# Latent attention relaid: 128-partition query tiles, rotary parts apart, heads in pairs, attended tokens scaled instead of probabilities

## The chip, the cores and the metric

One core of a Trainium2 chip. The metric is the device time of one execution in microseconds. In the profile PE is TensorE (PEld its weight loads), DVE is VectorE, ACT is ScalarE, POOL is GpSimd and SP is SyncE.

## What is computed

A decoder trunk of two layers, 256 tokens by 1024 features, float32. In a layer one input projection feeds three token mixers (a gated linear recurrence called LRU, retention, latent attention); their outputs are projected, weighted by sigmoid gates, added and projected again. A gated MLP with a short convolution follows. The part in question:

```python
q = (rmsnorm(cq, q_norm_g) @ w_uq).reshape(bsz, s, 8, 96)          # 64 plain + 32 rotary per head
q_nope, q_rope = q[..., :64], apply_rope(q[..., 64:])
k_nope, v = split((rmsnorm(ckv, kv_norm_g) @ w_ukv).reshape(bsz, s, 8, 128))
k_rope = apply_rope(kr)                                            # one rotary key for all heads
p = softmax(mask(q @ k.T * 96 ** -0.5))                            # 2 query blocks of 128
o = p @ v
merged = gates[0] * y_lru + gates[1] * y_ret + gates[2] * (o @ mla_wo)
```

## The kernel before, in words

Each engine has its own instruction list, written out by hand, and semaphores tie them together; there is no planner. Both layers run the same list in a loop.

**Weights.** Every weight block (mostly 128 x 2048 numbers, 1 MB) goes through a ring of three slots. SP loads block j into `raw` when the split of block j-3 is done; ACT copies it to `w_hi` in a rounded format (`split_hi`, L543) once PE is done with block j-3; DVE writes the rest, raw minus hi, to `w_lo` (`split_lo`, L1007). PE then makes each product of three matmuls, hi by lo, lo by hi and hi by hi (`mm3`, L1469). POOL sums the conditioning weights beside that and PE takes its sums in `ada_part` (L1505).

**Latent attention, first part.** After the retention scores PE runs `uq(0)` and `uq(1)`: each head's 96 query columns are one weight tile, so the eight heads are 8 x 3 x 3 = 72 matmuls of 256 tokens, laid out as 96 partitions per head in `AB`. Then `uk` (keys, 64 of the 96 partitions in `CD`), `head_means` and `head_scales` (the norm of retention) and the values into `EF`. On DVE the LRU recurrence (four scans, L1256) stands between the retention scores and the split of the key/value weights.

**Latent attention, second part.** Twelve steps m follow, four for each of the mixers in the order retention, LRU, attention. `merge_gate(m)` makes gate logits (48 matmuls), `merge_product(m)` projects a mixer's output (24 matmuls). DVE joins them in `merge(m)` (L1349, L1354). PE may overwrite the product's bank only after the merge of the step before (`mg_y`). Steps 0 to 7 also carry one attention head each, in this order on PE:

```python
for m in range(1, HEADS):
    merge_gate(m)            # m > 1
    mla_transpose(m - 1)     # waits for softmax_norm(m - 1) on ACT
    mla_score(m)
    merge_product(m)
    mla_av(m - 1)
```

The rotation of q and k is five float32 matmuls with a rotation matrix (`q_rotate(0..3)`, L1833, and `key_rotate`, L1757) around gates 0 and 1. DVE multiplies by the sine and cosine tables and adds, on 32 partitions, three operations of 512 numbers for each of the four pairs of heads (L1282, L1283, L1286), and `mla_score(0)` waits for the last. For each head DVE adds the mask (L1327), takes two maxima (L1329, L1330) and scales them (L1332); ACT takes the exponentials (L805, L807), DVE the reciprocal of the sums (L1337), ACT scales the probabilities (L813, L814), PE transposes three 128 x 128 tiles (L1773), ACT copies them out (L820), and `mla_av` (L1784, L1785) moves the probabilities past the values, so that the output has features on partitions. A float32 matmul is two instructions in the trace, a float32 transpose one.

ACT's and DVE's lists in a step m are the gate's tanh (L800), the softmax pieces, then the splits of the blocks three ahead. Block numbers: 15, 16 are uq, 17 is the key/value weights, 18 gate 0, 19 product weights 0, 20 gate 1, 21 gate 2, 22 product weights, 23 gate 3, 24 gate 4, 25 the product weights of the LRU, 26 gate 5 and so on, three blocks for two steps. In step 1 DVE also writes the low part of the LRU's output, `ob_lo` (L1387), which `merge_product(4)` waits for.

Of the kernel before, what the change touches and what calls it, by code (L numbers as in the profile page):

```python
# [21 lines left out]
P = 128  # L22
# [67 lines left out]
def trunk_kernel(nc, A, consts, out):  # L90
# [80 lines left out]
    with ctx:  # L171
# [38 lines left out]
        mx = sb("mx", [P, 2, 8])  # L210
# [101 lines left out]
        kr_ev, c_sq = sig("kr_ev", 1), sig("c_sq", 3)  # L312
# [3 lines left out]
        uq_ps, uq_ev = sig("uq_ps", 2), sig("uq_ev", 4)  # L316
        uk_ps, uk_ev = sig("uk_ps", 2), sig("uk_ev", 2)
        uv_ps, uv_ev = sig("uv_ps", 1), sig("uv_ev", 2)
        kt_ps, kt_t, kt_c, kt_sum, kt = sig("kt_ps", 1), sig("kt_t", 1), sig("kt_c", 1), sig("kt_sum", 1), sig("kt", 2)
        qt_ps, qt_t, qt_c, qt = sig("qt_ps", 4), sig("qt_t", 4), sig("qt_c", 4), sig("qt", 4)  # L320
        s_ps, s_m, s_max, s_neg = sig("s_ps", 8), sig("s_m", 8), sig("s_max", 8), sig("s_neg", 8)
        s_e, s_rc, s_n, s_tp, s_tev, s_av = (sig(n, 8) for n in ("s_e", "s_rc", "s_n", "s_tp", "s_tev", "s_av"))
# [24 lines left out]
        def gate_bank(m):  # L347

            return (3, 5)[m] if m < 2 else (4, 6)[m % 2]
# [6 lines left out]
        def kv_parts(t, j, packed):  # L356
# [7 lines left out]
            return [v[:, :, :, i] for i in range(2)]  # L364

# [138 lines left out]
        def _(act):  # L504
# [40 lines left out]
            def split_block(l, j):  # L545
# [9 lines left out]
                elif j == J[("ukv", 0)]:  # L555
# [4 lines left out]
                    a.then_inc(hi_ready.s, 1)  # L560
                elif j < NM:
# [80 lines left out]
            with act.Fori(0, L) as l:  # L642
# [49 lines left out]
                A_(kr[:], PS[:, 2, T:2 * T], ACT.Copy).then_inc(kr_ev.s, 1)  # L692
# [36 lines left out]
                def q_out(i):  # L729

                    if i % 2 == 0:
                        act.wait_ge(uq_ps.s, uq_ps.at(l, i // 2 + 1))
                    else:
                        product_done(act, l, J[("uq", i // 2)])
                    A_(AB[0:DQK, 2 * i:2 * i + 2, :].rearrange("p a b -> p (a b)"), PS[0:DQK, (2, 4, 6, 3)[i], :],
                       ACT.Copy).then_inc(uq_ev.s, 1)
# [8 lines left out]
                q_out(1)  # L745
                split_block(l, 18)
                ret_out(1)
                act.wait_ge(cn_lo.s, cn_lo.at(l, 1))
# [3 lines left out]
                q_out(2)  # L752
                q_out(3)
                split_block(l, 19)
                for i in range(2):
                    act.wait_ge(rv_ps.s, rv_ps.at(l, i + 1))
                    A_(var_sd[:, i, :], PS[:, (1, 2)[i], 0:8], ACT.Sqrt, bias=eps).then_inc(rv_sd.s, 1)

                def k_out(i):

                    act.wait_ge(uk_ps.s, uk_ps.at(l, i + 1))
                    for b in range(2):
# [1246 lines left out]
```

## Time and profile before

| | us |
|---|---|
| runs | 1103.14 median (1101.35 to 1103.78), 3 runs |
| the profiled execution | 1100.68, its span 1099.0 |
| PE busy | 1001.4 |
| DVE busy | 785.1 |
| ACT busy | 543.3 |
| POOL busy | 535.8 |
| mean granted TensorE clock | 0.974 of 2.4 GHz |

A matmul's row lasts until its result is out, so neighbouring matmuls overlap in the trace; the distance from start to start is what a matmul costs. In the windows, "PE busy" is the time covered by at least one of them, and the window's length minus that is PE's idle time.

### The profile page before, as it was taken

What the parts mean: (1) busy time and instruction counts of PE and PEld (TensorE: products, weight loads), DVE (VectorE), ACT (ScalarE), POOL (GpSimd) and SP (SyncE); (2) the same over time, 40 slices, a digit from 0 to 9 for tenths busy, and PEclk for the clock granted to TensorE, in tenths of its full rate; (3) what the DMA queues carried; (4) which work ended last, traced back from release to release, by engine and by line L of the source; (5) the groups of instructions that cost most, each with busy time, mean ns of one, the idle gap of its engine ahead of it and who ended that gap; (6) DMA issues with size and microseconds to landing.
All of it is one profiled execution on the core that took longest, in us unless ns stands there. A gap on an engine that the chain in (4) does not pass through costs nothing.

```text
span 1099.0 us, 19161 instructions
## 1 busy us (share of the span) xinstructions
PE 1001.4 (91%) x7074; PEld 927.4 (84%) x7074; DVE 785.1 (71%) x847; ACT 543.3 (49%) x697; POOL 535.8 (49%) x365
## 2 busy tenths in 40 slices
PE   5799999889998899999958999988999879999996
PEld 5789998788886899999947999878889769999995
DVE  4867678765678688888765867876666868766755
ACT  1543656545445555545444365744443564454554
POOL 0385675356664348888881477535566524000000
PEclk9999999999999799999988999999999979999998
DMA  9867655356555468677643765534665635555430
GB/s 300 306 192 239 210 187 184 108 173 210 168 196 192 134 219 264 227 247 227 232 156 106 231 198 177 191 115 154 205 194 187 220 110 179 192 178 187 169 115 39
DMA packets 140456, 206.56 MB, mean 188 GB/s; under 512 B 6289, under 2 KB 113115, under 8 KB 140251
## 3 DMA queue, kind: packets, MB, share of 16 engines
q1 hardware_dynamic: 128000, 161.76, 45.6%
q0 software_dynamic: 11520, 41.95, 11.2%
q10 hardware_dynamic: 859, 1.81, 0.4%
q8 instruction: 51, 0.84, 0.3%
q14 instruction: 26, 0.21, 0.1%
HBM read 204.45 MB, written 1.05 MB: 187 GB/s over the span
## 4 chain that ended last, share of the span: by engine, by line
PE 74%; DVE 12%; ACT 6%; issue 6%; DMA 1%; SPq 0%; DVEq 0%; ACTq 0%
PE banks L1469 63%; ACT w_hi L543 2%; PE banks L1495 2%; DMA AB<-in_ada_w 1%; DVE w_lo L1007 1%; PE banks L1520 1%; PE banks L1505 1%; DVE h L1058 1%; DVE AB L1283 1%; DVE mx L1332 1%; DVE h_lo L1065 1%; DVE x L1086 1%; PE banks L1587 1%; PE banks L1765 1%; ACT pbuf L807 1%
## 5 line engine op out<-in xcount | busy, mean ns | idle before, releaser
L1469 PE MATMUL banks<-h_lo,w_hi 128*128 128x256 f32 x1504 | 435.5, 290 | 7.9 <-DVE h_lo L1065 7.9
L1469 PE MATMUL banks<-h_hi,w_lo 128*128 128x256 f32 x1504 | 427.7, 284 | 0.0
L1469 PE MATMUL banks<-h_hi,w_hi 128*128 128x256 f32 x1504 | 427.5, 284 | 0.0
L1007 DVE TENSOR_TENSOR w_lo<-raw,w_hi 128x2048 fp32r<-128x2048 f32 (+1 forms) x87 | 244.9, 2820 | 84.4 <-ACT w_hi L543 84.2
L1469 PEld LDWEIGHTS banks<-h_lo,w_hi 128*128 128x128 f32 x1504 | 290.7, 193 | 12.1 <-issue 11.0
L1469 PEld LDWEIGHTS banks<-h_hi,w_lo 128*128 128x128 f32 x1504 | 290.9, 193 | 1.6 <-issue 1.4
L1469 PEld LDWEIGHTS banks<-h_hi,w_hi 128*128 128x128 f32 x1504 | 290.7, 193 | 0.0
L462 POOL TENSOR_TENSOR adp<-adw,cact 128x1024 f32<-128x1024 f32 x80 | 191.3, 2391 | 36.8 <-DMA adw<-in_ada_w 17.3
L543 ACT ACTIVATE w_hi<-raw 128x2048 fp32r<-128x2048 f32 (+1 forms) x87 | 162.2, 1873 | 64.7 <-PE banks L1469 57.4
L473 POOL TENSOR_TENSOR adacc<-adp 128x256 f32<-128x256 f32 x40 | 42.8, 1070 | 255.4 <-PE banks L1505 252.5
L1427 DVE TENSOR_TENSOR w_lo<-raw,w_hi 128x2048 fp32r<-128x2048 f32 x56 | 133.1, 2377 | 17.1 <-ACT w_hi L892 16.7
L468 POOL TENSOR_TENSOR adp<-adp 128x512 f32<-128x512 f32 x80 | 137.7, 1721 | 3.0 <-POOL adp L462 1.4
L1404 DVE SCALAR_TENSOR_TENSOR EF<-banks,cur,EF 128x254 f32<-128x254 f32 (+1 forms) x176 | 76.8, 478 | 75.5 <-ACT EF L873 71.3
L892 ACT ACTIVATE w_hi<-raw 128x2048 fp32r<-128x2048 f32 x56 | 107.2, 1913 | 46.3 <-PE banks L1469 46.3
L450 POOL DMA_DIRECT2D adw<-in_ada_w x80 | 63.1, 789 | 91.8 <-POOL adp L462 50.3
L873 ACT ACTIVATE EF<-banks,cur 128x256 f32<-128x256 f32 x88 | 44.9, 560 | 124.3 <-PE banks L1469 124.3
L1469 PE MATMUL banks<-w_hi,oa_lo 128*128 128x512 f32 x208 | 82.7, 398 | 2.7 <-DVE oa_lo L1422 2.7
L1469 PE MATMUL banks<-w_lo,oa_hi 128*128 128x512 f32 x208 | 82.2, 395 | 0.0
L1469 PE MATMUL banks<-w_hi,oa_hi 128*128 128x512 f32 x208 | 82.1, 395 | 0.0
L477 POOL TENSOR_TENSOR adp<-adp 128x256 f32<-128x256 f32 x40 | 52.6, 1315 | 3.1
L1469 PEld LDWEIGHTS banks<-w_hi,oa_lo 128*128 128x128 f32 x208 | 39.1, 188 | 12.0 <-DVE oa_lo L1422 3.6
L479 POOL TENSOR_TENSOR adacc<-adacc,adp 128x256 f32<-128x256 f32 x40 | 47.2, 1181 | 3.1
(273 smaller groups left out, 1503.0 us busy)
## 6 DMA issues: line engine op xcount, KB each, us to landing
raw<-in_w_in SPq DMA_DIRECT2D x52, 1024.0 KB, 6.4
raw<-in_ffn_w_up SPq DMA_DIRECT2D x44, 1024.0 KB, 5.8
adw<-in_ada_w POOLq DMA_DIRECT2D x80, 512.0 KB, 4.1
raw<-in_ffn_w_down SPq DMA_DIRECT2D x22, 1024.0 KB, 5.0
raw<-in_w_out SPq DMA_DIRECT2D x8, 1024.0 KB, 7.2
raw<-in_ret_wo SPq DMA_DIRECT2D x4, 1024.0 KB, 7.2
raw<-in_lru_wo SPq DMA_DIRECT2D x4, 1024.0 KB, 5.8
raw<-in_mla_wo SPq DMA_DIRECT2D x4, 1024.0 KB, 5.1
```

The lines of the kernel that those rows point to most:

```text
L450: pool.dma_start(adw[:, half], src(g)[:, 4 * half:4 * half + 4, :]).then_inc(adw_in[half], 16)
L462: nc.gpsimd.tensor_tensor(adp[:], weights, cb, ALU.mult).then_inc(ad_op, 1)
L468: nc.gpsimd.tensor_tensor(adp[:, 0:2], adp[:, 0:2], adp[:, 2:4], ALU.add).then_inc(ad_op, 1)
L477: nc.gpsimd.tensor_tensor(adp[:, 0], adp[:, 0], adp[:, 1], ALU.add).then_inc(ad_op, 1)
L479: nc.gpsimd.tensor_tensor(adacc[:, b], adacc[:, b], adp[:, 0], ALU.add).then_inc(acc_ready, 1)
L543: A_(dst, src, ACT.Copy).then_inc(hi_ready.s, 1)
L873: a = A_(EF[:, 2 * part + b, :], PS[:, 4 + part, T * b:T * b + T], ACT.Identity, scale=cur[:, bass.ds(i * 2 + col["tap2"] + NFF * (1 - par ...
L892: A_(w_hi[:, slot, :], raw[:, slot, :], ACT.Copy).then_inc(hi_ready.s, 1)
L1007: V.tensor_tensor(dst, whole, hi, ALU.subtract).then_inc(lo_ready.s, 1)
L1404: v = V.scalar_tensor_tensor(EF[:, 2 * part + b, d:T], PS[:, 4 + part, T * b:T * b + T - d], cur[:, bass.ds(i * 2 + col[f"tap{tap}"] + NFF ...
L1427: V.tensor_tensor(w_lo[:, slot, :], raw[:, slot, :], w_hi[:, slot, :].bitcast(F32), ALU.subtract).then_inc(lo_ready.s, 1)
L1469: ins = MM(ps, lhs, rhs, start=first and n == 0, stop=last and n == 2)
```

## The change

The query weights are packed as they are split: a block of four heads becomes 256 plain columns (four heads by 64) and 128 rotary columns (the two odd heads, then the two even ones), so a block is three tiles of 128. `AB[:, 0:4]` holds the plain parts, `AB[:, 4:6]` the rotary parts of all eight heads; `CD[:, 0:4]` the plain keys, `kr` the rotary key in all four groups of 32 partitions, and the values move to `CD[:, 4:8]`. A head's score is the sum of a 64-row matmul and a 32-row matmul. Heads go in pairs. The values are now the moving operand and the probabilities the weights, so the output has tokens on partitions; it is scaled by the reciprocal sums on DVE once, and transposed at the end (`mla_features`).

On PE, in order (L numbers are those of the kernel before where a line is kept):

```diff
@@ PE, first part
                 two_tiles(l, J[("g", 0)], 4)
+                pe.wait_ge(kt_t.s, kt_t.at(l, 1))
+                MM(PS[:, 2, 0:T], rot_m, lat[:, 0, :], start=True, stop=True).then_inc(kt_ps.s, 1)
...
-                pe.wait_ge(kr_ev.s, kr_ev.at(l, 1))
+                pe.wait_ge(kt.s, kt.at(l, 1))
                 two_tiles(l, J[("g", 1)], 2)
...
-                    for pair in range(2):
-                        n = 2 * i + pair
-                        sg, cnt = ((g_ev, 2), (lg_ev, 1), (lg_ev, 2), (ry_ev, 1))[n]
-                        pe.wait_ge(sg.s, sg.at(l, cnt))
-                        for b in range(2):
-                            cols = slice(DQK * (2 * pair + b), DQK * (2 * pair + b) + DQK)
-                            for k in range(QK):
...
+                    for t in range(3):
+                        ps = PS[:, (2, 6)[i], T * t:T * t + T] if t < 2 else PS[:, 4, T * i:T * i + T]
+                        cols = slice(P * t, P * t + P)
+                        for k in range(QK):
...
                 uk(1)
+                pe.wait_ge(qt_c.s, qt_c.at(l, 1))
+                pe.wait_ge(qt_t.s, qt_t.at(l, 1))
+                MM(PS[:, 4, :], rot_m, rot_tmp.rearrange("p a b -> p (a b)"), start=True, stop=True).then_inc(qt_ps.s, 1)
                 head_means(1)
@@ PE, second part
+                def mla_scores(p):
+                    if p >= 1:
+                        pe.wait_ge(s_tev.s, s_tev.at(l, p))
+                    for qs, ks, out_cols in ((slice(0, P), slice(0, P), slice(0, P)), (slice(P, T), slice(0, T), slice(P, 3 * P))):
+                        for h in (2 * p, 2 * p + 1):
+                            r = slice(64 * (h % 2), 64 * (h % 2) + 64)
+                            MM(PS[:, (3, 4)[h % 2], out_cols], AB[r, h // 2, qs], CD[r, h // 2, ks], start=True, stop=False)
+                        for h in (2 * p, 2 * p + 1):
+                            r = rope_rows(h)
+                            ins = MM(PS[:, (3, 4)[h % 2], out_cols], AB[r, 4 + h // 4, qs], kr[r, ks], start=False, stop=True)
+                    ins.then_inc(s_ps.s, 1)
+                def mla_av(p):
+                    pe.wait_ge(s_tev.s, s_tev.at(l, p + 1))
...
+                    for h in (2 * p, 2 * p + 1):
+                        pt, cols = ptb[:, h % 2, :], slice(64 * h, 64 * h + 64)
+                        MM(PS[:, 1, cols], pt[:, 0:P], v[:, 0, cols], start=True, stop=True)
+                        MM(PS[:, 2, cols], pt[:, P:2 * P], v[:, 0, cols], start=True, stop=False)
+                        ins = MM(PS[:, 2, cols], pt[:, 2 * P:3 * P], v[:, 1, cols], start=False, stop=True)
...
                 merge_gate(0)
-                key_rotate()
-                q_rotate(0)
-                q_rotate(1)
                 merge_gate(1)
-                q_rotate(2)
-                q_rotate(3)
                 merge_product(0)
...
+                mla_scores(0)
+                merge_product(1)
+                ada_part(ada_n, 6)
+                for m in range(2, HEADS):
+                    merge_gate(m)
+                    if m % 2 == 0:
+                        mla_transpose(m // 2 - 1)
+                        merge_product(m)
+                        mla_av(m // 2 - 1)
                     else:
+                        mla_scores(m // 2)
                         merge_product(m)
                         ada_part(ada_n, 6 + m // 2)
 
                 m = HEADS
                 merge_gate(m)
-                mla_transpose(m - 1)
-                mla_av(m - 1)
+                mla_transpose(3)
+                mla_av(3)
                 merge_gate(m + 1)
+                mla_features(0)
+                mla_features(1)
```

On DVE the scans leave the first part, the key is rotated before block 13's split, one `rotary_q_parts` and `rotary_q_sum` of 128 x 512 take the place of the twelve operations on 32 partitions, and the list of the steps becomes (`softmax_scores` is the mask add over both heads, two maxima over both, one scaling; `attended_low` reads the transposed output from the banks):

```diff
                 for m in range(12):
                     j = J[("gate", 0, 0)] + 3 * (m // 2)
-                    if 1 <= m < HEADS:
-                        softmax_scores(m)
...
+                    if m % 2 == 1 and m < HEADS:
+                        softmax_scores(m // 2)
+                    if m == 8:
+                        attended(0)
+                        attended(1)
+                        attended_low(0)
+                        attended_low(1)
+                    if m % 2 == 0:
                         split_block(l, j + RING)
+                    if m == 0:
+                        for t in range(4):
+                            lru_scan(t)
                     merge(m)
...
                     if m % 2 == 1:
                         split_block(l, j + RING + 1)
-                    if m % 2 == 1:
                         split_block(l, j + RING + 2)
-                    if m == 1:
-                        dve.wait_ge(l_ohi.s, l_ohi.at(l, 1))
...
+                    if m == 0:
+                        lru_out()
+                    if m == 3:
+                        lru_low()
```

On ACT the copy of `kr` (L692), two of the four query copies and two of the four key copies, the two broadcasts of the rotary key into `CD` (L789) and the scaling of the probabilities (L813, L814) go; both `uq` blocks are split in three pieces each instead of one (on DVE too). In the steps:

```diff
                     gate(m)
-                    if 1 <= m <= HEADS:
-                        transposed(m - 1)
-                    if m < HEADS:
-                        softmax_exp(m)
-                    if m in (5, 8):
-                        attended(m // 4 - 1)
+                    if m % 2 == 0 and 2 <= m <= HEADS:
+                        transposed(m // 2 - 1)
+                    if m % 2 == 1 and m < HEADS:
+                        softmax_exp(m // 2)
+                    if m == 9:
+                        attended(0)
+                        attended(1)
                     if m % 2 == 0:
                         split_block(l, j + RING)
                     else:
                         split_block(l, j + RING + 1)
-                    if m < HEADS:
-                        softmax_norm(m)
-                    if m % 2 == 1:
                         split_block(l, j + RING + 2)
+                    if m == 2:
+                        lru_high()
```

`softmax_exp(p)` is four exponentials, two for each head of the pair; `transposed(p)` copies 128 x 768 from two banks in one instruction.

## Rows read from the trace of the kernel before

**Rows 1.** The page: the span and the busy line of part 1.
```profile
span 1099.0 us, 19161 instructions
PE 1001.4 (91%) x7074; PEld 927.4 (84%) x7074; DVE 785.1 (71%) x847; ACT 543.3 (49%) x697; POOL 535.8 (49%) x365
```

**Rows 2.** Windows, layer 0 attention (the last: both together in layer 1).
```profile
core 0: us, PE busy (x) PEld busy (x) DVE busy (x) ACT busy (x) POOL busy (x), PEclk, DMA share, GB/s
162.70:183.75 21.05, 20.35 (x150) 17.62 (x149) 18.76 (x18) 13.39 (x20) 8.58 (x8) 1.00 0.61 200
183.75:309.08 125.33, 112.35 (x857) 104.30 (x856) 81.65 (x91) 57.41 (x91) 65.37 (x45) 0.99 0.50 163
212.51:239.65 27.14, 23.21 (x173) 21.85 (x172) 16.04 (x20) 13.53 (x24) 13.84 (x9) 0.94 0.63 195
688.41:834.71 146.30, 132.47 (x1004) 122.05 (x1003) 100.45 (x108) 70.68 (x110) 75.04 (x53) 0.99 0.53 169
```

**Rows 3.** Timeline of PE in layer 0: start, length; in brackets the idle time before.
```profile
203.52 0.49 PE L1764 MATMUL banks<-CD,AB 96*128 96x128 f32 x2 [1.35 <-DVE AB L1286]
...
210.12 0.55 PE L1773 MATMUL banks<-cst,pbuf 128*128 128x128 f32 x3 [2.80 <-ACT lat L800]
...
232.95 0.91 PE L1773 MATMUL banks<-cst,pbuf 128*128 128x128 f32 x3 [3.93 <-ACT pbuf L814]
...
305.78 0.39 PE L1469 MATMUL banks<-oa_lo,w_hi 128*128 128x256 f32 x1 [0.78 <-DVE EF L1354]
```

**Rows 4.** Critical chain, layer 0, pieces in order: start, length, what.
```profile
100.89 0.86 PE banks L1587 x2
...
136.56 2.32 PE banks L1650 x20
...
146.33 0.64 PE banks L1626 x4
146.97 0.22 PE banks L1627 x4
147.19 5.95 PE banks L1469 x48
...
245.65 0.33 PE banks L1773 x3
...
281.78 0.22 PE banks L1764 x2
282.00 0.43 PE banks L1765 x2
282.43 2.80 PE banks L1469 x24
285.24 0.58 PE banks L1784 x2
285.81 0.22 PE banks L1785 x2
...
286.57 5.88 PE banks L1469 x48
```

**Rows 5.** DVE, groups by line and form, 162 to 310 us.
```profile
L1007 DVE TENSOR_TENSOR w_lo<-raw,w_hi 128x2048 fp32r<-128x2048 f32 x16 | 43.4, 2715 | 16.6 <-ACT w_hi L543 16.6
...
L1256 DVE TENSOR_TENSOR_SCAN EF<-grow,h 128x256 f32<-128x256 f32 x4 | 4.8, 1256 | 0.0
...
L1327 DVE TENSOR_TENSOR pbuf<-banks,cst 128x384 f32<-128x384 f32 x8 | 4.5, 556 | 9.9 <-PE banks L1765 9.7
L1354 DVE SCALAR_TENSOR_TENSOR EF<-lat,banks 128x512 f32<-128x512 f32 x6 | 4.1, 682 | 8.2 <-PE banks L1469 8.2
...
L1387 DVE TENSOR_TENSOR ob_lo<-EF,ob_hi 128x1024 fp32r<-128x1024 f32 x1 | 1.7, 1749 | 0.0
```

**Rows 6.** ACT, the same stretch.
```profile
L543 ACT ACTIVATE w_hi<-raw 128x2048 fp32r<-128x2048 f32 x17 | 32.4, 1904 | 6.9 <-PE banks L1469 6.9
...
L807 ACT ACTIVATE pbuf<-pbuf,mx,lat_rc 128x256 f32<-128x256 f32 x8 | 4.7, 586 | 0.0
```

More of the change, by code:

```diff
@@ L784, in _ @@
                     A_(flat2(oa_hi, i), flat2(tmp, i), ACT.Copy).then_inc(r_ohi.s, 1)
-                k_out(1)
-                act.wait_ge(kt_sum.s, kt_sum.at(l, 1))
-                for half in range(2):
-                    A_(CD[64:96, 4 * half:4 * half + 4, :], kr[64:96, :].unsqueeze(1).to_broadcast([32, 4, T]),
-                       ACT.Copy).then_inc(kt.s, 1)
                 def gate(m):
@@ L822, in attended, with softmax_exp @@
-                def attended(i):
-                    act.wait_ge(s_av.s, s_av.at(l, 4 * i + 4))
-                    if i == 0:
-                        product_done(act, l, J[("gate", 0, 3)])
-                    A_(flat2(oa_hi, i), PS[:, 2, :], ACT.Copy).then_inc(m_ohi.s, 1)
+                def softmax_exp(p):
+                    act.wait_ge(s_neg.s, s_neg.at(l, p + 1))
+                    for b in range(2):
+                        for c, cols in enumerate((slice(0, P), slice(P, 3 * P))):
+                            a = A_(pbuf[:, b, cols], pbuf[:, b, cols], ACT.Exp, scale=lat_rc[:, c:c + 1],
+                                   bias=sneg[:, c, b:b + 1], accum_out=ssum[:, c, 2 * p + b:2 * p + b + 1])
+                    a.then_inc(s_e.s, 1)
@@ new lines, in transposed, with attended @@
+                def transposed(p):
+                    act.wait_ge(s_tp.s, s_tp.at(l, p + 1))
+                    if p >= 1:
+                        act.wait_ge(s_av.s, s_av.at(l, p))
+                    A_(ptb[:], PS[:, 3:5, 0:384], ACT.Copy).then_inc(s_tev.s, 1)
+                def attended(c):
+                    act.wait_ge(m_tp.s, m_tp.at(l, c + 1))
+                    product_done(act, l, J[("gate", 0, 3)])
+                    A_(oa_hi[:, :, P * c:P * c + P], PS[:, (3, 4)[c], :].rearrange("p (a b) -> p a b", a=4),
+                       ACT.Copy).then_inc(m_ohi.s, 1)
@@ L828, in merged_hi, with lru_high @@
+                def lru_high():
+                    act.wait_ge(l_o.s, l_o.at(l, 1))
+                    A_(ob_hi[:, 0:4, :], EF[:, 4:8, :], ACT.Copy).then_inc(l_ohi.s, 1)
                 def merged_hi(i):
@@ new lines, in lru_out, with lru_low @@
+                def lru_out():
+                    dve.wait_ge(l_h.s, l_h.at(l, 4))
+                    dve.wait_ge(lg_ev.s, lg_ev.at(l, 2))
+                    V.tensor_tensor(EF[:, 4:8, :], EF[:, 4:8, :], EF[:, 0:4, :], ALU.mult).then_inc(l_o.s, 1)
+                def lru_low():
+                    dve.wait_ge(l_ohi.s, l_ohi.at(l, 1))
+                    V.tensor_tensor(ob_lo[:, 0:4, :], EF[:, 4:8, :], ob_hi[:, 0:4, :].bitcast(F32),
+                                    ALU.subtract).then_inc(l_olo.s, 1)
@@ L1788, in merge_y, with mla_features @@
+                def mla_features(c):
+                    pe.wait_ge(s_n.s, s_n.at(l, c + 1))
+                    o = AB[:, 4 + 2 * c:6 + 2 * c, :].rearrange("p a b -> p (a b)")
+                    for t in range(4):
+                        ins = nc.tensor.transpose(PS[:, (3, 4)[c], P * t:P * t + P], o[:, P * t:P * t + P], ident)
+                    ins.then_inc(m_tp.s, 1)
                 def merge_y(b, i, wj):
```

311 lines of the change are left out of this document (138 added, 173 removed).

## The prediction

> **What bounds the kernel.** PE is busy for 91% of the span [rows 1], so I looked for the time in which it is not, stage by stage. In the windows of the attention stage [rows 2], the first part of layer 0 takes 21.05 us with 0.70 idle, the second part 125.33 us with 125.33 - 112.35 = 12.98 idle. Layer 1's whole stage takes 146.30 us, against 21.05 + 125.33 = 146.38 in layer 0, so each number below counts twice. The timeline shows where PE waits [rows 3]: 1.35 us for the last rotation of q on DVE, 2.80 us in step 1 for the first head's softmax, 3.93 us in step 3 for ACT's scaled probabilities, and 0.78 us for the merge of step 8, four of the eight waits in it. After the wait of 3.93 us the granted clock fell: the window 212.51 to 239.65 has 0.94 [rows 2], that is some 3.3 us at 1.2 instead of 2.4 GHz, in which half the work was done, a loss of 1.6 us. So besides its work the second part loses 12.98 + 1.6 = 14.6 us per layer. Outside this stage the change touches nothing but the rotary key.
>
> **The prices of PE's work** [rows 4]. A 256-token matmul of `mm3` costs 5.88 / 48 = 0.12 us (24 of a product, 2.8 us). A float32 rotation of 512 columns costs 0.86 us, a transpose 0.33 / 3 = 0.11. One head's score of 96 rows costs 0.22 + 0.43 = 0.65 us. Two heads' retention scores, with the same 384 columns each but on 64 rows at different partitions, cost 0.64 + 0.22 = 0.86 together, not 1.3: they run beside each other in part, down to 0.86 / 8 = 0.108 us an instruction. The gate behind them took 5.95 instead of 5.88 us, which I take for the change of tile, 0.09 us with rounding.
>
> **The change, part by part, per layer.** (minus is a gain)
> - Query projection: 72 matmuls become 2 x 3 x 9 = 54. 18 x 0.12 = -2.2 us.
> - Rotation of q: four matmuls become one, -3 x 0.86 = -2.6. The key's matmul only moves ahead.
> - Scores: eight times 0.65 (5.2 us) become four pairs of 16 instructions, half on 64 and half on 32 rows. No row shows 32-row tiles. If each pair of tiles runs fully side by side a pair costs 2 x 0.65 = 1.3 us; if nothing does, 4 x 0.65 + 4 changes of tile x 0.09 = 3.0. The nearest row is retention's: 16 x 0.108 = 1.7 and 0.36 for the changes, 2.1 us. 4 x 2.1 - 5.2 = +3.2.
> - Values: a head costs 0.58 + 0.22 = 0.80 us now, 6.4 in all. After it, each head is six instructions with full weights and 64 moving columns; the nearest row, with one column, has 2.32 / 20 = 0.116 us. 48 x 0.116 = 5.6. That is -0.8; between instructions of 0.10 and 0.15 the total is 4.8 to 7.2.
> - `mla_features`: eight transposes, +0.9. The softmax's 24 transposes stay.
> Together 2.2 + 2.6 + 0.8 - 3.2 - 0.9 = 1.5 us less work.
>
> **The waits.** I walk through the lists with durations from the rows, from PE's view.
> First part: the scans leave DVE (4 x 1.2 us [rows 5]), so the key/value split is early; the rotary parts of q (two operations of about 0.7) follow uq(1) and are needed only behind 12 + 12 + the key matmuls and a head mean, 4.6 us later. Hidden. Idle 0.70 becomes about 0.4. The three-piece splits of uq cost perhaps 0.5 us more on ACT and DVE, hidden behind the two-tile products of 5.95 us. The rotary key's two products and sum (0.4 us each) go into DVE's wait for the next block and behind the retention scores; PE needs the sum only after 20 small matmuls of 2.32 us [rows 4]. If that cover were gone they would cost 1.2.
> - Gate 0 to scores: q and k are long ready; 1.35 us goes.
> - Product 1 waits for merge(0), and on DVE that now stands behind block 21's split and the four scans. From gate 0's end: tanh 0.6, high part 1.9 [rows 6], low part 2.7 [rows 5], scans 4.8, merge 0.7 [rows 5]: 10.7 us. PE gets there after gate 1, product 0, scores: 5.9 + 2.8 + 2.1 = 10.8. On the edge; I count 0.3.
> - Step 1's wait of 2.80 goes, since the softmax of a pair now has a product and a gate as cover (2.8 + 5.9 us against about 2.3 on DVE and 2.2 on ACT). Product 2 then waits for block 22: 0.5.
> - Step 3's wait of 3.93 goes too, since no scaling on ACT stands between. **But a new one comes at product 4.** It needs `ob_lo` (`lru_low`), which is now last in DVE's step 3, behind the splits of blocks 25 and 26. From the end of product 3: the scores ended 2.9 us before it, DVE's part for the pair takes 2.3 (the mask add of 768 numbers about 0.95, from 0.556 for 384 [rows 5], maxima 1.1, scaling 0.2), ACT's four exponentials 2.2 (0.59 for the longer [rows 6]): +1.6. High part of 25 at 3.5, low parts 2.7 each to 6.2 and 8.9, `lru_low` 1.75 to 10.7. PE arrives after 0.5 of `ada_part`, 5.9 of gate 4 and 0.7 of transposes: 7.1. The wait is 3.6 us, like today's 3.93, so I count the clock loss of 1.6 us again.
> - Step 8: the values of the last pair wait for ACT's copy of 768 columns, 0.8. Merge(8) stays at 0.8, gate 9 may wait 0.2.
> Sum: 0.3 + 0.5 + 3.6 + 0.8 + 0.2 + 0.8 = 6.2 idle and 1.6 for the clock, 7.8 against 14.6. With 0.3 from the first part, -7.1 us.
>
> Per layer 1.5 + 7.1 = 8.6 us, twice 17.2. The profiled execution had 1100.7 us, which gives 1083.5; it lies 2.5 us under the median of the three runs, which would give 1085.9. I say **1084.5 us**.
>
> ACT loses sixteen scalings and the broadcasts of a layer, DVE nine of the twelve operations of the rotation. That is worth only what it does to the waits above; it is not added. The transfers are not in the way: the second part uses 0.50 of the DMA engines [rows 2], and at some 9 us less it would use 0.54.
>
> **A rule that speaks against it.** The gate behind 64-row scores lost 0.09 us [rows 4], and the sum goes by that. The Trainium skill, "TensorEngine Tiling (Array Packing)", section "Key Properties", says that changing the tiling mode, not just the tile, drains TensorE. By that rule the four changes in each pair's scores would each wait for the matmul before to come out.
>
> **Rivals.**
> 1. More is gained (15%). The two heads' tiles run fully beside each other (1.3 a pair, -3.2 a layer) and splits a few tenths shorter than their mean leave under 3 us of wait at product 4, with no fall of the clock (-2.5). For it: retention's pairs overlap, and the wait of 2.80 us was followed by matmuls at full clock. Against: 0.108 us an instruction looks like a floor. 1084.5 - 2 x 5.7 = 1073.
> 2. Less is gained (15%). The 32-row tiles do not overlap with anything (+3.6 a layer) and the DVE chain ahead of product 4 and product 1 runs 1 us later each (the 2.7 us of a split is a mean, and several stand in a row), +2. 1084.5 + 11 = 1096.
> 3. The stage is bound by the supply of split blocks, not by the softmax (4%): every gate would wait for its block and the saved time would come back as waits for `w_lo`. DVE is busy 81.65 of 125.33 us [rows 2], against it. 1101 to 1105.
> 4. Slower (6%): each change between 128-, 64- and 32-row tiles drains the array. The place is `mla_scores`, four changes in each of eight pairs, 32. To cancel 17.2 us each would have to cost 0.54 us more than the 0.09 I count. At one matmul's whole latency (a row lasts some 0.3 us from start to end [rows 3]: 0.39 for the first) it is 32 x 0.3 = 10 us, still 1094; the two-pass float32 tiles would have to drain between each other too, 128 times at 0.15 = 19, which gives 1104 to 1108.
>
> **How the numbers follow.** The forecast has 60%, with its own range 1079 to 1091 (clock fall or not, 3; values and scores to either side, 3 to 5). The range of 1074 to 1096 takes in most of rivals 1 and 2 and leaves about 2 in 10 out. A measurement of this kernel tells 0.2%, 2.2 us, from no change: faster 0.90, same 0.04, slower 0.06.
>
> **What would show it.** Right: the sum of PE's idle time in the second part near 6 us, one wait of 3 to 4 us before product 4 released by DVE's `ob_lo`, no wait before the first scores, some 2.1 us per pair of scores, uq in 3.3 us each, about 8 us less from uq(0) to gate 10 in each layer. Wrong: waits of over 1 us before other products, released by `w_lo` or by merges; a pair of scores over 3 us; a clock under 0.9 in a window where it was 1.00.

## The result, and the profile of the changed kernel

The changed kernel takes 1082.86 us, the median of four runs (1081.25 to 1085.35), where the kernel before, run beside it, takes 1102.7. The ratio is 0.9826, with a 95% interval of 0.9813 to 0.9839: faster by 1.7%. The forecast was 1084.5. The profiled execution had 1083.08 us and a span of 1081.4. The page begins with the span, then busy time by engine, then the shares of the chain that ended last:

```profile
span 1081.4 us, 19149 instructions
PE 997.6 (92%) x7138; PEld 928.0 (86%) x7138; DVE 765.2 (71%) x795; ACT 522.5 (48%) x651; POOL 555.3 (51%) x365
...
PE 82%; DVE 9%; ACT 4%; issue 3%; DMA 1%; SPq 0%; DVEq 0%; ACTq 0%
```

Beside [rows 1], PE's busy time fell by only 3.8 us of the 17.6 that the span lost. DVE lost 20 and ACT 21 us of work, while POOL's same 365 instructions took 19.5 us longer. So most of the gain, 13.8 us, is idle time of PE.

The windows of the stage from uq(0) to gate 10, the first and second part in layer 0, then all of it in layer 1 (columns as in [rows 2]):

```profile
165.57:184.50 18.93, 18.91 (x134) 16.09 (x132) 14.16 (x16) 12.01 (x16) 11.38 (x8) 1.00 0.73 242
184.50:302.69 118.19, 110.56 (x902) 105.43 (x902) 75.38 (x59) 48.09 (x68) 77.50 (x49) 0.99 0.54 174
680.70:817.81 137.11, 129.48 (x1034) 121.69 (x1033) 90.64 (x74) 60.10 (x83) 88.66 (x57) 0.99 0.56 182
```

Layer 0 takes 18.93 + 118.19 = 137.12 us instead of 146.38, layer 1 137.11 instead of 146.30: 9.3 and 9.2 us less. The idle time of the second part is 118.19 - 110.56 = 7.63 instead of 12.98, that of the first 0.02 instead of 0.70. The whole span splits without a rest: uq(0) starts 2.87 us later, layer 0's stage is 9.26 shorter, the stretch from there to layer 1's uq(0) 1.32 shorter (379.33 to 378.01), layer 1's stage 9.19 shorter, the end 0.70 shorter; together -17.60. Of the 2.87 us, some 0.9 come before any edit, and 0.4 to 0.6 are the rotary key's matmul, which now stands there. Most of the rest is a slower clock that layer 0 alone shows: the window from 140 to 160 us has a granted clock of 0.92 where the kernel before had 1.00, and layer 1 loses nothing there.

The timeline of PE in layer 0, with all waits of the second part:

```profile
201.70 0.39 PE L1503 MATMUL banks<-oa_lo,w_hi 128*128 128x256 f32 x1 [0.47 <-DVE h L1386]
...
213.21 0.38 PE L1503 MATMUL banks<-oa_lo,w_hi 128*128 128x256 f32 x1 [1.53 <-DVE w_lo L1018]
...
239.31 0.58 PE L1503 MATMUL banks<-ob_lo,w_hi 128*128 128x256 f32 x1 [3.95 <-DVE ob_lo L1299]
...
285.63 0.44 PE L1819 MATMUL banks<-CD,ptb 128*128 128x64 f32 x2 [0.90 <-ACT ptb L827]
...
299.74 0.39 PE L1503 MATMUL banks<-oa_lo,w_hi 128*128 128x256 f32 x1 [0.78 <-DVE EF L1391]
```

They stand before product 1, product 2, product 4, the values of the last pair and product 9, and sum to 7.63 us. The waits for q, for the first head's softmax and for the scaled probabilities [rows 3] are gone; the merge's 0.78 is as it was. Layer 1 has the same five (0.49, 1.50, 3.95, 0.90, 0.78). After the long one the clock fell. This is the window of product 4's matmuls, where a product at full clock takes 2.94 us:

```profile
239.31:243.59 4.28, 4.28 (x24) 4.28 (x25) 2.51 (x1) 0.00 (x0) 3.75 (x2) 0.65 1.00 296
```

And this is one pair's scores on PE, then the first matmul of the next product:

```profile
223.31 0.49 PE L1801 MATMUL banks<-CD,AB 64*128 64x128 f32 x4
223.73 0.49 PE L1804 MATMUL banks<-kr,AB 32*128 32x128 f32 x4
224.15 0.70 PE L1801 MATMUL banks<-CD,AB 64*128 64x256 f32 x4
224.79 0.70 PE L1804 MATMUL banks<-kr,AB 32*128 32x256 f32 x4
225.42 0.38 PE L1503 MATMUL banks<-oa_lo,w_hi 128*128 128x256 f32 x1
```

The starts are to be read here, since a duration has the array's latency in it: 225.42 - 223.31 = 2.11 us a pair, as forecast. What the 2.11 is made of is another matter, and took three runs.

### The profile page after: what moved, and what is told of

It is laid out like the page before. It is cut to its first block, busy times and chain, and to the rows that moved or that the text cites. A ratio compares the mean times of both kernels' runs of the same rounds, so it can differ in the third digit from the quotient of the medians.

```text
span 1081.4 us, 19149 instructions
## 1 busy us (share of the span) xinstructions
PE 997.6 (92%) x7138; PEld 928.0 (86%) x7138; DVE 765.2 (71%) x795; ACT 522.5 (48%) x651; POOL 555.3 (51%) x365
## 4 chain that ended last, share of the span: by engine, by line
PE 82%; DVE 9%; ACT 4%; issue 3%; DMA 1%; SPq 0%; DVEq 0%; ACTq 0%
PE banks L1503 70%; DVE w_lo L1018 2%; PE banks L1529 2%; ACT w_hi L565 1%; DMA AB<-in_ada_w 1%; DVE EF L1290 1%; PE banks L1554 1%; DVE h L1074 1%; PE banks L1539 1%; DVE h_lo L1081 1%; ACT pbuf L819 1%; DVE x L1102 1%; PE banks L1621 1%; PE banks L1640 1%; PE banks L1804 1%
## 5 line engine op out<-in xcount | busy, mean ns | idle before, releaser
L1018 DVE TENSOR_TENSOR w_lo<-raw,w_hi 128x2048 fp32r<-128x2048 f32 x83 | 237.1, 2872 | 69.6 <-ACT w_hi L565 69.3
L565 ACT ACTIVATE w_hi<-raw 128x2048 fp32r<-128x2048 f32 x83 | 156.8, 1907 | 70.8 <-PE banks L1503 60.8
L1461 DVE TENSOR_TENSOR w_lo<-raw,w_hi 128x2048 fp32r<-128x2048 f32 x56 | 133.1, 2376 | 17.3 <-ACT w_hi L903 16.8
L490 POOL TENSOR_TENSOR adp<-adp 128x512 f32<-128x512 f32 x80 | 134.3, 1678 | 3.0 <-POOL adp L484 1.4
L903 ACT ACTIVATE w_hi<-raw 128x2048 fp32r<-128x2048 f32 x56 | 107.1, 1913 | 46.6 <-PE banks L1503 46.6
L499 POOL TENSOR_TENSOR adp<-adp 128x256 f32<-128x256 f32 x40 | 61.2, 1530 | 3.1
L813 ACT ACTIVATE lat<-banks 128x512 f32<-128x512 f32 x24 | 14.4, 598 | 98.4 <-PE banks L1503 98.3
L501 POOL TENSOR_TENSOR adacc<-adacc,adp 128x256 f32<-128x256 f32 x40 | 59.7, 1493 | 3.1
```

The lines of the kernel that those rows point to most:

```text
L490: nc.gpsimd.tensor_tensor(adp[:, 0:2], adp[:, 0:2], adp[:, 2:4], ALU.add).then_inc(ad_op, 1)
L499: nc.gpsimd.tensor_tensor(adp[:, 0], adp[:, 0], adp[:, 1], ALU.add).then_inc(ad_op, 1)
L501: nc.gpsimd.tensor_tensor(adacc[:, b], adacc[:, b], adp[:, 0], ALU.add).then_inc(acc_ready, 1)
L565: A_(dst, src, ACT.Copy).then_inc(hi_ready.s, 1)
L903: A_(w_hi[:, slot, :], raw[:, slot, :], ACT.Copy).then_inc(hi_ready.s, 1)
L1018: V.tensor_tensor(dst, whole, hi, ALU.subtract).then_inc(lo_ready.s, 1)
```

## The experiments

The theory: each wait of the second part is set by one late operation in the queues of DVE or ACT, and the long one takes the clock with it; PE's work does the rest. The rival: DVE and ACT bound this part together and hand a removed wait on. "Stage" below is uq(0) to gate 10, 137.1 us in both layers of the changed kernel.

**The low part of the recurrent output one step earlier.**

```diff
-                    if m == 3:
+                    if m == 2:
                         lru_low()
```

> The changed kernel with one line moved: DVE's lru_low, the low part of the LRU's output, goes from the end of step 3 to the end of step 2, where DVE idles for 6 us. Theory (PE's walk sets the end; what product 4 waits for is its place in DVE's list): the wait of 3.95 us before product 4 and the slow clock behind it (24 matmuls in 4.45 instead of 3.1 us) go in both layers, 2 x (3.95 + 1.35) = 10.6 us, 1082.9 to about 1072. Block 25's low part ends 1.2 us before PE arrives, so it does not take the wait over. Rival (the stage is bound by the supply of split blocks): product 4 or a later product waits for w_lo in its place, and the time stays within 2 us of 1083.

Measured: 1074.37 us, 0.9739 of before (0.9704 to 0.9774); the stages take 131.56 and 131.48 us. Product 4 follows the transposes at once:

```profile
233.93 0.82 PE L1811 MATMUL banks<-cst,pbuf 128*128 128x128 f32 x6
234.50 0.36 PE L1503 MATMUL banks<-ob_lo,w_hi 128*128 128x256 f32 x1
```

The 24 matmuls take 2.94 us. The other four waits are as before (0.48, 1.52, 0.90, 0.78). The wait and the clock's loss sum to 3.95 + 1.34 to 1.51 = 5.3 to 5.5 us, and the stages are 5.6 us shorter each. So the new wait was real, nothing took its place, and it cost 11.2 us in the two stages. By the medians the kernel gains 8.5 us, 2 less than the forecast; at least part of that stands behind layer 1's stage, where the profiled execution took 1.9 us longer for the same work (265.5 against 263.6 us).

**Three more rotations of q.**

```diff
+                for _ in range(3):
+                    MM(PS[:, 4, :], rot_m, rot_tmp.rearrange("p a b -> p (a b)"), start=True, stop=True)
                 MM(PS[:, 4, :], rot_m, rot_tmp.rearrange("p a b -> p (a b)"), start=True, stop=True).then_inc(qt_ps.s, 1)
```

> The changed kernel with the rotation matmul of q written four times instead of once (the same result, as often as the kernel before rotates). Theory (PE's work in the first part is on the path to the end): 3 x 0.86 = 2.6 us more per layer, 1082.9 to about 1088. Rival (the work saved there is covered by what PE waits for afterwards): 0 to 1 us more.

Measured: 1088.32 us, 0.9866 (0.9837 to 0.9894). The stages take 139.66 and 140.61 us. In layer 0 that is 3 x 0.86 = 2.6 more; layer 1 has 0.8 us on top, where product 4 took 5.28 instead of 4.45 us at the slow clock (the profiled execution, 1092.69 us, was the longest of the four). The rotations' price is on PE's path in full.

**Probabilities scaled again.** ACT scales a pair's probabilities between its two splits of blocks, the transposes wait for that, and the later scaling on DVE is by one.

```diff
                         split_block(l, j + RING + 1)
+                        if m < HEADS:
+                            softmax_norm(m // 2)
                         split_block(l, j + RING + 2)
...
                 def mla_transpose(p):
-                    pe.wait_ge(s_e.s, s_e.at(l, p + 1))
+                    pe.wait_ge(s_nm.s, s_nm.at(l, p + 1))
```

> The changed kernel with the probabilities scaled again: for each pair DVE takes the reciprocals after the merge, ACT scales the four pieces between the splits of the two blocks, the transposes wait for that; the attended tokens are multiplied by one, so that work is the same. Theory (the pairs have a product and a gate as cover; the scaling's removal alone is worth little): ACT's 1.8 us per pair delays the second block of a step, so product 4 waits some 1.5 us longer and gate 9 some 0.5, the transposes of step 2 some 0.2: 1 to 2.5 us per layer, 1085 to 1088. Rival (taking the scaling off the way to the transposes is the main source of the gain): the waits of 2.8 and 3.9 us before transposes come back, 8 us or more in all, 1091 or more.

Measured: 1083.39 us, 0.9827 (0.9793 to 0.986), and the same five waits, product 4's at 3.97, in stages of 137.3 and 137.1 us. Both expectations were too high: the scaling costs nothing here. I looked for why, since 1.5 us of ACT work ahead of block 26's split should have made the low part of the recurrent output later. The timeline of DVE in the changed kernel (without the scaling), the low parts of blocks 25 and 26:

```profile
231.84 2.29 DVE L1018 TENSOR_TENSOR w_lo<-raw,w_hi 128x2048 fp32r<-128x2048 f32 x1 [2.61 <-ACT w_hi L565]
...
234.05 3.37 DVE L1018 TENSOR_TENSOR w_lo<-raw,w_hi 128x2048 fp32r<-128x2048 f32 x1
```

and POOL's operation beside the second:

```profile
233.27 2.00 POOL L490 TENSOR_TENSOR adp<-adp 128x512 f32<-128x512 f32 x1
```

The same operations with the scaling, where all times lie 0.93 us earlier:

```profile
234.09 2.40 DVE L1029 TENSOR_TENSOR w_lo<-raw,w_hi 128x2048 fp32r<-128x2048 f32 x1 [0.90 <-ACT w_hi L566]
...
232.33 2.01 POOL L491 TENSOR_TENSOR adp<-adp 128x512 f32<-128x512 f32 x1
```

Without the scaling the low part starts 0.9 us sooner and then stands: it takes 3.37 us and ends 2.15 us after POOL's sum (235.27 to 237.42). With it, it starts when the sum is nearly over, takes 2.40 us, and ends 2.15 us after it as well (234.34 to 236.49). The delay on ACT fell into time in which DVE could not work anyway. That fits the Trainium skill, "SBUF — State Buffer", section "SBUF: two separate sides", which calls the port pair that VectorE and GpSimd share an exclusive lock. The two ends at 2.15 us agree with it, and so does the whole trace of the changed kernel: 67 low parts of 2048 numbers begin during a sum of POOL, at any point of it, and all end 2.15 to 2.25 us after it, while the 45 that touch none take 2.28 or 2.29 us. It works the other way too: POOL's 256-column sums (L499, L501) that begin during a low part end 0.6 us after it, and there are 26 of these instead of 16, which is where POOL's longer busy time comes from (61.2 + 59.7 us instead of 52.6 + 47.2). Eight more low parts begin 0.01 to 0.56 us ahead of a sum of POOL and still end 2.16 us after it, so by the records it is not always the one that starts first that runs first. No run here moved POOL's work by itself.

**The four scans ahead of the split of block 17, as they were.**

```diff
+                for t in range(4):
+                    lru_scan(t)
                 split_block(l, 17)
                 split_block(l, 18)
...
-                    if m == 0:
-                        for t in range(4):
-                            lru_scan(t)
                     merge(m)
```

> The changed kernel with the four LRU scans back in front of the split of the key/value weights, as in the kernel before. Theory: product 1 no longer waits for merge(0) (0.47 us per layer), but in the first part the key/value split, the rotary parts of q and the variances come up to 4.8 us later, beyond their cover: waits of 1 to 2 us per layer before the keys, the rotation or the head scales. In sum 0.5 to 3 us slower, 1083.5 to 1086. Rival (the scans' place decides the first part, where the kernel before had them too): 1081 to 1083, no wait in the first part over 0.7.

Measured: 1086.52 us, 0.9849 (0.982 to 0.9877). The first part now waits 1.39 us for the key/value split and 1.24 for the rotary q, and the waits before product 1 and product 2 are gone. In layer 1 it waits once, 2.08 us, for the same split. So moving the scans is worth 3.7 us by the medians, a little over what I expected, though it also makes the 0.47 and part of the 1.53 us. The idle time of the stages hardly differs, 8.28 and 7.73 us against 7.65 and 7.63; what makes them longer, 138.87 and 140.19 us, is mostly the clock. Product 4 took 5.28 us in layer 0, and behind the 2.08 us of layer 1 the window of 10 us has a granted clock of 0.66.

**The exponentials behind the split.**

```diff
-                    if m % 2 == 1 and m < HEADS:
-                        softmax_exp(m // 2)
...
                         split_block(l, j + RING + 1)
+                        if m < HEADS:
+                            softmax_exp(m // 2)
                         split_block(l, j + RING + 2)
```

> In the odd steps ACT makes the high part of the first block ahead of the pair's exponentials. Theory: DVE's low part of that block starts up to 1.9 us earlier, so the wait of 1.5 us before product 2 goes, and that before product 4 stays or falls by up to 1 us, since the second block's low part starts where it does now: 2 x 1.5 to 2 x 2.5, 1078 to 1080 us. Rival (the transposes become late because the exponentials end 1.9 us later): a wait before the transposes of pairs 0 to 2, and 1083 us or more.

Measured: 1080.45 us, 0.9796 (0.9777 to 0.9815). Product 2's wait is gone and product 4's is 3.72, 1.76 us less idle; but product 4 took 5.28 us, 1.0 and 0.8 more at the slow clock, so the stages end at 136.34 and 136.03. No wait came before the transposes: the exponentials have slack.

**A shorter cover for the softmax.**

```diff
                 for m in range(2, HEADS):
-                    merge_gate(m)
                     if m % 2 == 0:
                         mla_transpose(m // 2 - 1)
+                    merge_gate(m)
+                    if m % 2 == 0:
                         merge_product(m)
```

> On TensorE the transposes of pairs 0, 1 and 2 stand ahead of the next gate instead of behind it, so that only a product and a part of ada (3.4 us) cover a pair's softmax (some 4.5 us from the end of the scores to the last exponential). Theory (the cover that the pairs' order gives is what removed the softmax waits): a wait of 1.0 to 1.5 us for the probabilities before each of the three. In the steps of pairs 0 and 1 it only takes the place of the wait that product 2 and product 4 have anyway, for blocks whose times hang on DVE; pair 2 has none to take: 1.2 us a layer, 1085.5 us. Rival (waits add up): 2 x 3 x 1.2, 1090 us. If no wait appears before the transposes, the cover by the gate wasn't needed.

Measured: 1089.13 us, 0.9878 (0.9857 to 0.9899), nearer the rival's figure. The waits of its second part up to the last pair:

```profile
198.88 0.39 PE L1503 MATMUL banks<-oa_lo,w_hi 128*128 128x256 f32 x1 [0.47 <-DVE h L1386]
204.70 0.88 PE L1811 MATMUL banks<-cst,pbuf 128*128 128x128 f32 x6 [2.35 <-ACT pbuf L819]
...
227.91 0.87 PE L1811 MATMUL banks<-cst,pbuf 128*128 128x128 f32 x6 [1.22 <-ACT pbuf L819]
237.18 0.38 PE L1503 MATMUL banks<-ob_lo,w_hi 128*128 128x256 f32 x1 [2.64 <-DVE ob_lo L1299]
...
255.58 0.87 PE L1811 MATMUL banks<-cst,pbuf 128*128 128x128 f32 x6 [1.22 <-ACT pbuf L819]
```

The mechanism is as expected. A wait of 2.35, 1.22 and 1.22 us came before each transpose; it took the place of product 2's wait and of 1.3 us of product 4's, and only the third was all new. The sum of waits is 9.58 instead of 7.63 us, and the stages take 139.06 and 139.16, 2.0 more each. That is 4 of the 6 us. The rest lies outside the stage: this execution began 2.6 us earlier with uq(0) and then needed 382.84 us from gate 10 to layer 1's uq(0), where the changed kernel needed 378.01 for the same work. Two windows of 20 us at the same distance behind gate 10, first of the changed kernel, then of this one:

```profile
322.69:342.69 20.00, 20.00 (x88) 16.07 (x87) 18.14 (x11) 8.98 (x10) 11.85 (x8) 1.00 0.71 230
642.69:662.69 20.00, 20.00 (x163) 19.31 (x161) 14.59 (x14) 14.74 (x26) 14.63 (x11) 1.00 0.47 149
```

```profile
322.05:342.05 20.00, 20.00 (x81) 15.97 (x80) 15.85 (x9) 8.99 (x10) 11.85 (x8) 0.91 0.73 239
642.05:662.05 20.00, 20.00 (x157) 19.28 (x156) 13.57 (x13) 18.05 (x28) 14.29 (x10) 0.97 0.58 181
```

PE is busy throughout in all four, but the granted clock is 0.91 and 0.97 here and 1.00 there. The edit does not reach this place, and the kernels compared below have 378 to 383 us there too. Within the stage the verdict is plain: without the gate as cover, softmax waits return; with it there are none.

**64 rows for the rotary products.** The 32-row matmuls become 64-row ones, so each score also has another head's rotary product in it.

```diff
-                            r = rope_rows(h)
+                            r = slice(64 * (h % 2), 64 * (h % 2) + 64)
```

> Changed computation: the rotary product of a head's scores runs over 64 rows instead of 32, so a score also has another head's rotary product in it; the number of instructions and columns is unchanged, and no change between 64 and 32 rows is left (the changes between 128 and 64 rows stay). My forecast's step counted 0.36 us a pair for four changes of tile: two of them would go, 8 pairs x 0.18 = 1.4 us, 1081.5 us in all. Reading of the trace after the change (each instruction of 128 columns takes 0.105 us on 64 and on 32 rows alike): nothing, 1083 us, and a pair still takes 2.11 us. Rival (a change of the row height drains the array at 0.3 us or more): 8 x 4 x 0.3 = 5 us less in total at least, 1078 or under.

Measured: 1086.2 us, 0.9836 (0.9808 to 0.9864), not told apart from the changed kernel. But a pair is much shorter:

```profile
222.35 0.49 PE L1801 MATMUL banks<-CD,AB 64*128 64x128 f32 x4
222.67 0.39 PE L1804 MATMUL banks<-kr,AB 64*128 64x128 f32 x4
222.90 0.60 PE L1801 MATMUL banks<-CD,AB 64*128 64x256 f32 x4
223.33 0.60 PE L1804 MATMUL banks<-kr,AB 64*128 64x256 f32 x4
223.86 0.38 PE L1503 MATMUL banks<-oa_lo,w_hi 128*128 128x256 f32 x1
```

1.51 instead of 2.11 us. Both readings of my own (two changes at 0.09 us, and no cost at all) were wrong, the second most of all. The rival's was right: eight pairs save 4.8 us of PE's time, near its 5, though the product written there, 8 x 4 x 0.3, is 9.6. The whole gained nothing: of 4 x 0.6 = 2.4 us a layer, 0.6 came back as a longer wait at product 1 (1.08 instead of 0.47) and 0.8 to 1.0 as a longer stretch of slow clock at product 4 (5.24 us at a granted 0.51). Each stage is 0.8 to 0.9 us shorter, and the stretch between the two 4.6 us longer, as in the run before.

This run had undone two things: the change of row height, and that a head's rotary rows lie in the other half of the partitions than its plain rows. Two runs told these apart.

**The halves.** Both parts of a head in the same half, 64 and 32 rows kept.

```diff
-                odd, even = (v[:, :, 2 * P + 64 * i:2 * P + 64 * i + 64].rearrange("p k (h n) -> p k h n", h=2) for i in range(2))
+                odd, even = (v[:, :, 2 * P + 64 * i:2 * P + 64 * i + 64].rearrange("p k (h n) -> p k h n", h=2) for i in (1, 0))
...
-            r = (64 if h % 2 == 0 else 0) + 32 * (h % 4 // 2)
+            r = 64 * (h % 2) + 32 * (h % 4 // 2)
```

> In the changed kernel a head's rotary rows (32) lie in the other half of the partitions than its plain rows (64). The run with 64-row rotary matmuls took 1.51 us a pair instead of 2.11, but it had undone two things: the change of row height and that change of half. Here the heights stay (64 and 32 rows), and the packed columns of the query weights and the rows are swapped so that both parts of a head lie in the same half; what is computed is the same. If the change of height costs (0.2 us each, three in a pair beside the one behind it): 2.11 us a pair still, 1083 us. If the change of half costs, because a head's second matmul then waits for the first of the other tile: 1.5 us a pair, 8 x 0.6 = 4.8 us less work, of which at least 0.6 a layer comes back as a wait at product 1: 1079 to 1080 us.

Measured: 1083.09 us, 0.9837 (0.9807 to 0.9866). A pair still starts 2.11 us before what follows (222.59 to 224.70). The half does not matter. On top of the best kernel (below) the same swap says the same:

> The same swap on top of the kernel with the three changes of order (1068.7 us), which has no waits left that would take the gain up but 0.9 and 0.8 us a layer. Height reading: 1068.7 us, 2.11 us a pair. Half reading: 1.5 us a pair, 4.8 us less, 1064 us, a little more if product 1 waits for the first merge again.

Measured: 1071.37 us, 0.9716 (0.9699 to 0.9732), 2.11 us a pair, stages of 129.02 and 129.09, as without the swap (129.03 and 129.08). The 2.7 us between the two medians are not in the stages; in the profiled executions, 1.7 us apart, uq(0) starts 1.9 us later with the swap.

**The three orders together.** The low part after product 2, the exponentials behind the split (both as above), and the first merge ahead of the last scan:

```diff
                     if m == 0:
-                        for t in range(4):
+                        for t in range(3):
                             lru_scan(t)
                     merge(m)
+                    if m == 0:
+                        lru_scan(3)
```

> Three changes of order in the queues of the second part: the low part of the recurrent output after product 2 instead of product 3, the high part of the odd steps' first block ahead of the exponentials on ACT, the first merge ahead of the last scan on DVE. Theory (the waits of 3.95, 1.5 and 0.47 us a layer are each set by one late operation, and the fall of the clock to 1.2 GHz goes with the wait of 3.95): 2 x (3.95 + 1.35 + 1.5 + 0.47) = 14.6 us less than the changed kernel, 1068.5 us; waits of 0.9 before the last pair's values and 0.8 before product 9 stay. Rival (DVE and ACT are the bound of this part and hand the waits on): only the 8.7 us that the move of the low part alone gave, 1074 us, with waits of 1 us or more before gates or products 6 and 8.

Measured: 1068.7 us, 0.9687 (0.9667 to 0.9707), against an expected 1068.5. Its windows, the stage's two parts in layer 0:

```profile
162.95:181.88 18.93, 18.93 (x135) 16.40 (x134) 14.47 (x16) 12.02 (x16) 13.36 (x8) 1.00 0.85 275
181.88:291.98 110.10, 108.42 (x901) 103.83 (x901) 77.15 (x59) 47.88 (x68) 74.89 (x49) 1.00 0.57 183
```

The idle time is 1.68 us, the two waits of 0.90 and 0.78 us, and the clock stays at 1.00. Each stage is 8.1 us shorter. DVE is busy 77.15 of 110.10 us and handed nothing on, so the rival falls.

**Two changes of height instead of three.** On the kernel just told of, the second query tile starts its sum with the 32-row products, so that a pair goes 64, 32, 32, 64 rows.

```diff
-                            MM(PS[:, (3, 4)[h % 2], out_cols], AB[r, h // 2, qs], CD[r, h // 2, ks], start=True, stop=False)
...
+                        if first:
+                            nope(True)
+                            rope(False)
+                        else:
+                            rope(True)
+                            ins = nope(False)
```

(`nope(start)` and `rope(start)` issue the 64-row and the 32-row matmuls of both heads, with `stop=not start`.)

> On top of the kernel with the three changes of order (1068.7 us): for the second query tile the 32-row matmuls start the sum and the 64-row ones end it, so that the order in a pair is 64, 32, 32, 64 rows, with two changes between heights inside the pair instead of three and the same number of instructions. Height reading: each change costs 0.2 us, so a pair takes 1.9 instead of 2.11 us and the whole 1067 us. Half reading (the same halves as before in each sum): 2.1 us a pair, 1068.7 us.

Measured: 1069.98 us, 0.9708 (0.9692 to 0.9724), not told apart from 1068.7. The pair:

```profile
220.41 0.49 PE L1805 MATMUL banks<-CD,AB 64*128 64x128 f32 x4
220.84 0.92 PE L1811 MATMUL banks<-kr,AB 32*128 32x128 f32 x8
221.69 0.70 PE L1805 MATMUL banks<-CD,AB 64*128 64x256 f32 x4
222.32 0.39 PE L1505 MATMUL banks<-oa_lo,w_hi 128*128 128x256 f32 x1
```

1.91 us, 0.20 less, with the same sixteen instructions and one change of height fewer. The stages take 128.59 and 128.47 us, 0.4 and 0.6 less, near the three pairs' 3 x 0.2; the first pair took 2.08, with a short wait for the first merge behind it. The runs together: 2.11 with three changes inside a pair, 1.91 with two, 1.51 with none. The last two begin and end a pair with the same tiles, so 0.40 us goes with two changes, and the first adds 0.20 for the third. A change between 64 and 32 rows costs 0.20 us on the mean, 0.6 a pair, 4.8 in the kernel.

## Why the prediction was right, step by step

The mechanism held, and so did the size: 1084.5 forecast, 1082.86 measured; from the profiled execution 1083.5 against 1083.08. That the sum fits so closely is in part luck. Idle time in the stage fell by 6.0 and 6.2 us in the two layers where I had 7.1, and PE's busy time by 3.2 and 3.0 where I had 1.5 less work.

- **Where the time went.** Forecast 8.6 us a layer; the stage lost 9.3 and 9.2, of which 0.43 is the key's rotation (256 columns, half of q's 0.86), now ahead of it. Another 0.6 of the busy time is the values, below; the rest is not assigned. PE's waits, 6.2 forecast, are 7.63: product 1 0.47 (0.3), product 2 1.53 (0.5), product 4 3.95 (3.6), last values 0.90 (0.8), product 9 0.78 (0.8), gate 9 none (0.2). **Product 2's is the mis-sized term.** I had charged each low part at the mean of 2.7 us, but they range from 2.3 us to 3.8. The one that product 2 waits for is of the long kind, 1.0 us more than the mean, which is the whole error. It is one of the eight told of above, 2.16 us behind the end of a sum of POOL:

```profile
209.30 3.78 DVE L1018 TENSOR_TENSOR w_lo<-raw,w_hi 128x2048 fp32r<-128x2048 f32 x1 [3.42 <-ACT w_hi L565]
...
209.60 1.32 POOL L490 TENSOR_TENSOR adp<-adp 128x512 f32<-128x512 f32 x1
```

A wait of over 1 us released by `w_lo` was one of my signs of being wrong; it came true in this one place. At product 4 the two low parts, 2.29 and 3.37 us, happen to sum to nearly the 5.4 that I had charged.

- **The clock.** 1.6 us forecast at product 4; 1.34 and 1.51 in the two layers (4.28 and 4.45 against 2.94 us). Other runs had 2.3 (5.21 to 5.28 us). Product 2's wait of 1.53 and the 2.35 of the shorter cover had no slow matmuls behind them, the 2.64 us of that same run had (4.47 us at 0.62), and so had the 2.08 us with the scans back. So the length of the wait alone does not decide it.
- **The first part.** 0.4 us of idle forecast, 0.02 measured. The run with the scans back shows what hid it: 1.39 and 1.24 us of waits appear.
- **uq and rotation.** A uq takes 27 x 0.12 us as forecast; the run with three rotations more puts some 0.85 us each on the path (2.54 us in layer 0).
- **Scores.** 2.11 us a pair, forecast 2.1, by the wrong parts. I took 16 x 0.108 for the matmuls and 0.36 for four changes, where there are five: three between 64 and 32 rows and those from and to 128. In fact the two heads' tiles run side by side, which is the 1.3 us of my lower bound (in the 64-row run four instructions of 128 columns take 0.23 us, four of 256 columns 0.43), and the rest is changes: 1.51 with those from and to 128 rows alone, and 0.60 for three between 64 and 32. The retention scores [rows 4] fit the same parts: their 0.64 + 0.22 us are 0.65 for the instructions and some 0.2 for the changes to 64 rows and back, so 0.108 us an instruction was no floor.
- **The changes of height.** The three kernels show 0.20 us for each, and that decides the split of the 2.11 us. The rule of the Trainium skill ("TensorEngine Tiling (Array Packing)", "Key Properties"), that a change of tiling mode drains the array, agrees with this price, though no row shows the drain itself. Rival 4 had its mechanism right and its size wrong. I priced it at one latency of 0.3 and needed 0.54 over my 0.09 for it to win; and it does not apply between tiles of one height, where the second head's runs beside the first's. Its last sum is also off: 1094 and 19 more are 1113, not 1104 to 1108.
- **Values and features.** 1.26 us a pair of heads, 5.0 a layer, forecast 5.6; eight transposes 0.87, forecast 0.9.
- **The scaling.** I gave its removal no term of its own. The run that puts it back agrees: nothing. What removed the softmax waits is the order in pairs, a product and a gate between scores and transposes; with the gate taken out of it 1.2 to 2.4 us come back at each.

Rival 1 had the full overlap, which is there, and is paid back by changes of height. Rival 2's late DVE chain is there at product 2 with 1 us, not at product 4. Rival 3 is excluded by the kernel with three orders changed, in which the same supply carries a stage 8 us shorter.

What stays open is why equal work outside the stage differs. From gate 10 of layer 0 to uq(0) of layer 1, profiled executions needed 378.0 us (changed kernel), 378.1 (low part earlier), 382.6 (64 rows), 382.7 (three orders) and 382.8 (shorter cover), the others between 378.4 and 382.6; the kernel before, 379.3. It is the granted clock of a few windows, and no run was made to explain it. That is why I compare stages where an edit is worth under 5 us.

## What to carry to other kernels

When a change takes a wait away, walk the queue behind it and ask which operation is late next: here 4 us moved from the softmax to `ob_lo`, and one line moved in DVE's list then gave nearly half as much again as the whole change had. Do not charge an operation of DVE at its mean before looking at how its durations spread: here they hang on where POOL's operations lie. Order small matmuls so that the row height changes least, and price a change of height at 0.2 us. Before charging work on ACT or DVE to the path, look whether its consumer was held by something else at that time.

## What the runs showed of the hardware that I had not expected

- A change between 64-row and 32-row tiles costs 0.20 us on PE (2.11, 1.91 and 1.51 us a pair with three, two and no such changes). Which half of the partitions a tile lies in costs nothing. Two heads' 64-row tiles with 256 columns run fully side by side: four instructions in 0.43 us, as long as two of one head's [rows 4].
- A subtraction of 128x2048 on DVE takes 2.29 us alone and 3.37 when it starts during POOL's sum; two such, started 0.97 us apart against POOL's operation, both end 2.15 us after that operation ends, and the 67 of the changed kernel that begin during one end 2.15 to 2.25 us after it.
- After nearly the same wait of 3.7 to 4.0 us, 24 matmuls took 4.28 to 4.47 us in some cases and 5.21 to 5.28 in others, instead of 2.94. A gain of 1.8 us of waiting ahead of such a fall was half lost in it.
